# Layer norm statistics of the convolution summed as columns, with filler products between the sums and an earlier load of the silu table

## The reference, cut to what matters

```python
def layer_norm(x, g, b):
    xf = x.astype(jnp.float32)
    mu = jnp.mean(xf, axis=-1, keepdims=True)
    var = jnp.mean(jnp.square(xf - mu), axis=-1, keepdims=True)
    y = (xf - mu) * lax.rsqrt(var + EPS)
    return (y * g.astype(jnp.float32) + b.astype(jnp.float32)).astype(x.dtype)

def conformer_conv_module(h, w_in, b_in, w_dw, b_dw, ln_g, ln_b, w_out, b_out):
    u = h @ w_in + b_in
    a, gate = jnp.split(u, 2, axis=-1)
    u = a * jax.nn.sigmoid(gate)
    u = lax.conv_general_dilated(...) + b_dw        # 31 taps, depthwise, causal
    u = jax.nn.silu(layer_norm(u, ln_g, ln_b))
    return u @ w_out + b_out
```

## Time and profile before

| | |
|---|---|
| median of three runs | 2198.0 us |
| profiled execution, device time | 2200.97 us |
| its span, first to last instruction | 2199.2 us |
| TensorE matmul busy | 2184.2 us, 99% |
| VectorE, ScalarE, GpSimd busy | 1406.0, 991.3, 202.9 us |
| mean granted TensorE clock | 0.998 of full |

### The profile page before, as it was taken

How to read it: one execution, slowest core, us unless ns; L and a number is a source line. 1 busy time by engine, 2 the same in 40 slices (tenths; PEclk the granted TensorE clock), 3 DMA queues, 4 the chain that set the end, 5 groups by cost and what they waited for, 6 DMA issues and landing times.

```text
span 2199.2 us, 32498 instructions
## 1 busy us (share of the span) xinstructions
PE 2184.2 (99%) x13012; PEld 1927.1 (88%) x13012; DVE 1406.0 (64%) x1314; ACT 991.3 (45%) x821; POOL 202.9 (9%) x105
## 2 busy tenths in 40 slices
PE   8999999999999999999999999999999999999998
PEld 8999888888888888888888888888888888888887
DVE  6999786555555555557766767675565555555655
ACT  6666554443344433444354344444443344433444
POOL 7999000000000000000000000000000000000000
PEclk9999999999999999999999999999999999999999
DMA  9665456455545465545544435555555554555452
GB/s 247 183 175 168 138 188 221 176 198 190 190 174 208 172 210 177 207 175 184 194 158 145 143 119 207 194 189 191 191 179 203 180 200 175 200 188 188 174 210 77
DMA packets 250043, 400.46 MB, mean 182 GB/s; under 512 B 6407, under 2 KB 72143, under 8 KB 249935
## 3 DMA queue, kind: packets, MB, share of 16 engines
q1 hardware_dynamic: 249406, 398.74, 53.4%
q0 software_dynamic: 352, 0.56, 0.1%
q10 hardware_dynamic: 208, 0.07, 0.0%
HBM read 397.24 MB, written 2.10 MB: 182 GB/s over the span
## 4 chain that ended last, share of the span: by engine, by line
PE 92%; DVE 4%; issue 2%; DVEq 1%; DMA 1%; ACT 0%; SPq 0%; ACTq 0%
PE bank L1281 55%; PE bank L1283 27%; PE bank L1562 4%; DVE bank L932 2%; PE bank L1354 2%; PE bank L1547 1%; PE bank L1624 1%; DMA raw<-in_conv_w_in 1%; DVEq L910 0%; PE bank L1368 0%; DVE bank L926 0%; PE bank L1499 0%; PE bank L1371 0%; DVE bank L913 0%; PE bank L1489 0%
## 5 line engine op out<-in xcount | busy, mean ns | idle before, releaser
L1281 PE MATMUL bank<-x_both,w_hi 128*128 128x512 f32 x3328 | 1159.0, 395 | 0.0
L775 DVE TENSOR_TENSOR w_lo<-raw,w_hi 128x2048 fp32r<-128x2048 f32 x343 | 779.2, 2290 | 528.9 <-ACT w_hi L486 528.7
L486 ACT ACTIVATE w_hi<-raw 128x2048 fp32r<-128x2048 f32 x374 | 707.4, 1909 | 630.0 <-PE bank L1283 601.5
L1283 PE MATMUL bank<-x_both,w_lo 128*128 128x256 f32 x3328 | 923.8, 278 | 0.0
L1281 PEld LDWEIGHTS bank<-x_both,w_hi 128*128 128x128 f32 x3328 | 625.4, 188 | 146.9 <-issue 1.1
L1281 PE MATMUL bank<-h_both,w_hi 128*128 128x512 f32 x1872 | 651.1, 394 | 0.4 <-DVE h_both L976 0.4
L1283 PEld LDWEIGHTS bank<-x_both,w_lo 128*128 128x128 f32 x3328 | 626.2, 188 | 0.1
L1283 PE MATMUL bank<-h_both,w_lo 128*128 128x256 f32 x1872 | 519.5, 278 | 0.0
L1281 PEld LDWEIGHTS bank<-h_both,w_hi 128*128 128x128 f32 x1872 | 351.1, 188 | 82.9 <-issue 0.5
L1283 PEld LDWEIGHTS bank<-h_both,w_lo 128*128 128x128 f32 x1872 | 351.7, 188 | 0.0
L1354 PE MATMUL bank<-x_both,w_hi 128*128 128x256 f32 x960 | 173.2, 283 | 0.0
(11 more groups left out here) (222 smaller groups left out, 1183.0 us busy)
## 6 DMA issues: line engine op xcount, KB each, us to landing
raw<-in_ffn_w_gate_up SPq DMA_DIRECT2D x176, 1024.0 KB, 4.9
raw<-in_ffn_w_down SPq DMA_DIRECT2D x88, 1024.0 KB, 5.1
raw<-in_gla_w_in SPq DMA_DIRECT2D x48, 1024.0 KB, 5.2
raw<-in_conv_w_in SPq DMA_DIRECT2D x32, 1024.0 KB, 6.1
raw<-in_conv_w_out SPq DMA_DIRECT2D x16, 1024.0 KB, 5.2
raw<-in_gla_w_out SPq DMA_DIRECT2D x16, 1024.0 KB, 7.1
x_rows<-in_x SPq DMA_DIRECT2D x4, 512.0 KB, 6.4
out<-out_rows SPq DMA_DIRECT2D x4, 512.0 KB, 3.1
```

What stands on the lines that cost most here:

```text
L486: nc.scalar.activation(w_hi[k][:, :, :], raw[k][:, :, :], ACT.Copy).then_inc(hi_done, 1)
L775: nc.vector.tensor_tensor(w_lo[k][:, :, :], raw[k][:, :, :], w_hi[k][:, :, :].bitcast(F32), ALU.subtract).then_inc(lo_done, 1)
L1281: mm(to, w_hi[k][:, kt, cols], xx[:, :, k0 + kt, :], start=(first and kt == 0), stop=False, skip_group_check=True)
L1283: ins = mm(to[:, 0:T], w_lo[k][:, kt, cols], xx[:, 0, k0 + kt, :], start=False, stop=(last and kt == 3), skip_group_check=True)
```

## The change

- `column_sums` takes the place of the products with ones. The tile is now the stationary operand, in two halves of 128 tokens, and one column of ones is the moving one; each product gives a 128x1 column of token sums. Ahead of the two products come `idle` filler products (default 1, and 0 for the last two sums). The shift becomes a sum of its own with a column of fours.
- Mean, square, variance, root and reciprocal work on 128x2 elements (`ln_cols`).
- Two diagonal matrices (`neg_mean_diag`, `rstd_diag_ln`, each two 128x128 halves) are made on VectorE, and TensorE turns each into a row form again by a product with the 128x128 ones, twice each, into two PSUM banks: one copy is read by VectorE directly, the other is copied to SBUF by ScalarE (`rows_kept`).
- ScalarE issues a one-element silu straight after the root, so that the table is loaded there.
- `join_last(0)` moves two taps earlier; `ln_center(1)` moves ahead of the first scaling; the fillers after the sums are regrouped.

```diff
@@ last convolution tile, and the statistics on VectorE
-                    if n == JOIN_AT + 4 and last:
+                    if n == JOIN_AT + 2 and last:
                         join_last(0)
...
-            nc.vector.scalar_tensor_tensor(out=sq_sum[:, :], in0=shift[:, :], scalar=4.0 * P, in1=y_total,
-                                           op0=ALU.mult, op1=ALU.add).then_inc(mean_done, 1)
+            nc.vector.tensor_scalar(nm, y_total, -1.0 / D, None, ALU.mult).then_inc(mean_done, 1)
             dve.wait_ge(mean_done, 1)
-            nc.vector.scalar_tensor_tensor(out=rstd[:, :], in0=sq_sum[:, :], scalar=1.0 / D ** 2, in1=sq_sum[:, :],
-                                           op0=ALU.mult, op1=ALU.mult).then_inc(mean_done, 1)
+            nc.vector.tensor_tensor(msq, nm, nm, ALU.mult).then_inc(mean_done, 1)
             dve.wait_ge(mean_done, 2)
             dve.wait_ge(stat_done, STAT[1])
-            nc.vector.scalar_tensor_tensor(out=rstd[:, :], in0=sq_total, scalar=1.0 / D, in1=rstd[:, :],
+            nc.vector.scalar_tensor_tensor(out=var, in0=sq_total, scalar=1.0 / D, in1=msq,
                                            op0=ALU.mult, op1=ALU.subtract).then_inc(var_done, 1)
+            for a in range(2):
+                ins = nc.vector.tensor_scalar(neg_mean_diag[:, a * P:(a + 1) * P], ident[:, :], nm[:, a:a + 1], None, ALU.mult)
+            ins.then_inc(mean_diag, 1)
+            dve.wait_ge(root_done, 2)
+            nc.vector.reciprocal(rs, var).then_inc(rstd_done, 1)
+            dve.wait_ge(rstd_done, 2)
+            for a in range(2):
+                ins = nc.vector.tensor_scalar(rstd_diag_ln[:, a * P:(a + 1) * P], ident[:, :], rs[:, a:a + 1], None, ALU.mult)
+            ins.then_inc(ln_diag, 1)
@@ ScalarE
-            nc.scalar.activation(rstd[:, :], rstd[:, :], ACT.Sqrt, bias=eps[:, 0:1]).then_inc(root_done, 1)
+            nc.scalar.activation(ln_cols[:, 2, :], ln_cols[:, 2, :], ACT.Sqrt, bias=eps[:, 0:1]).then_inc(root_done, 1)
+            nc.scalar.activation(rstd_tok[:, 0:1], eps[:, :], ACT.Silu)
+            scalar.wait_ge(rows_done, 2)
+            nc.scalar.activation(sq_sum[:, :], neg_mean_row[1], ACT.Copy).then_inc(rows_kept, 1)
             for t in range(KT):
...
+                if t == 0:
+                    scalar.wait_ge(rows_done, 4)
+                    nc.scalar.activation(rstd[:, :], rstd_row[1], ACT.Copy).then_inc(rows_kept, 1)
@@ TensorE
-            def add_square(square, signal, count, start=False, stop=False):
+            def column_sums(to, tile, start=False, stop=False, by=None, idle=1):
+
+                busy(tap_first[:, 0:P], idle)
+                by = ones[:, 0:1] if by is None else by
+                for a in range(2):
+                    ins = mm(to[:, a:a + 1], tile[:, a * P:(a + 1) * P], by, start=(start and a == 0), stop=stop,
+                             skip_group_check=True)
+                return ins
+
+            def add_square(square, signal, count, start=False, stop=False, idle=1):
 
                 pe.wait_ge(signal, count)
-                return mm(sq_total, ones[:, :], square, start=start, stop=stop)
-
+                return column_sums(sq_total, square, start, stop, idle=idle)
+
+            pe.wait_ge(tap_done, TAP_STEPS * (KT - 1) - LAST_TAPS[0] + 1)
             add_square(sq_late[:, 4, :], y_sq, 4, start=True)
             add_square(sq_late[:, 5, :], y_sq, 5)
+            pe.wait_ge(consts, 21)
+            column_sums(y_total, shift, start=True, by=four[:, :])
             pe.wait_ge(ysum_done, KT - 1)
-            mm(y_total, ones[:, :], y_sum[:, :], start=True, stop=False)
+            column_sums(y_total, y_sum)
             for tile in range(2):
                 add_square(sq_early[:, tile, :], sq_pre, 3)
             pe.wait_ge(join_done, KT)
-            mm(y_total, ones[:, :], act[:, KT - 2, :], start=False, stop=False)
+            column_sums(y_total, act[:, KT - 2, :])
             add_square(sq_late[:, 6, :], y_sq, 6)
             pe.wait_ge(join_done, KT + 2)
-            mm(y_total, ones[:, :], act[:, KT - 1, :], start=False, stop=True).then_inc(stat_done, 1)
-            add_square(sq_late[:, 7, :], y_sq, 7, stop=True).then_inc(stat_done, 1)
-            for signal, count, n in ((var_done, 1, 2), (root_done, 2, 7), (rstd_done, 2, 1), (z_done, 1, 2), (xn_done, KT + 1, 2)):
+            column_sums(y_total, act[:, KT - 1, :], stop=True, idle=0).then_inc(stat_done, 1)
+            add_square(sq_late[:, 7, :], y_sq, 7, stop=True, idle=0).then_inc(stat_done, 1)
+            busy(tap_first[:, 0:P], 4)
+            pe.wait_ge(mean_diag, 1)
+            for row in neg_mean_row:
+                mm(row, ones[:, :], neg_mean_diag[:, :], start=True, stop=True).then_inc(rows_done, 1)
+            pe.wait_ge(ln_diag, 1)
+            for row in rstd_row:
+                mm(row, ones[:, :], rstd_diag_ln[:, :], start=True, stop=True).then_inc(rows_done, 1)
+            busy(slot[1][:, 2, 0:P], 2)
+            for signal, count, n in ((z_done, 1, 2), (xn_done, KT + 1, 2)):
                 pe.wait_ge(signal, count)
                 busy(slot[1][:, 2, 0:P], n)
```

More of the change, by code:

```diff
@@ L141, in trunk @@
         sq_early = sb("sq_early", [P, 8, T], 72 * K)
-        last_diag = [sb(f"last_diag{j}", [P, P], 80 * K + 512 * j) for j in range(sum(LAST_TAPS))]
-        assert sum(LAST_TAPS) <= 18
+        last_diag = [sb(f"last_diag{j}", [P, P], 80 * K + 512 * j) for j in range(18)]
+        last_diag += [sb(f"last_diag{18 + j}", [P, P], 95 * K + 512 * j) for j in range(2)]
+        assert sum(LAST_TAPS) <= len(last_diag)
+        ln_cols = sb("ln_cols", [P, 4, 2], 93 * K)
+        four = sb("four", [P, 1], 93 * K + 64)
+        neg_mean_diag = sb("neg_mean_diag", [P, T], 91 * K)
+        rstd_diag_ln = sb("rstd_diag_ln", [P, T], 92 * K)
         y_sum = sb("y_sum", [P, T], 69 * K)
@@ L182, in trunk @@
         y_last = [slot[1][:, 2, :], slot[1][:, 0, :]]
-        y_total, sq_total = bank[:, 0, 0:T], bank[:, 1, 0:T]
+        y_total, sq_total = bank[:, 0, 0:2], bank[:, 1, 0:2]
+        neg_mean_row, rstd_row = [bank[:, b, 0:T] for b in (4, 6)], [bank[:, b, 0:T] for b in (5, 7)]
         raw_in = [sem(f"raw_in{i}") for i in range(RING)]
@@ L229, in trunk @@
         var_done = sem("var_done")
+        mean_diag = sem("mean_diag")
+        ln_diag = sem("ln_diag")
+        rows_done = sem("rows_done")
+        rows_kept = sem("rows_kept")
         cent_done = sem("cent_done")
@@ L406, in _ @@
             nc.gpsimd.memset(shift_w[:, :], -1.0 / P).then_inc(consts, 1)
+            nc.gpsimd.memset(four[:, :], 4.0).then_inc(consts, 1)
             for c in range(2):
@@ L953, in _ @@
             join_last(1)
+            nm, msq, var, rs = (ln_cols[:, i, :] for i in range(4))
             dve.wait_ge(stat_done, STAT[1] - 1)
-            nc.vector.scalar_tensor_tensor(out=sq_sum[:, :], in0=shift[:, :], scalar=4.0 * P, in1=y_total,
-                                           op0=ALU.mult, op1=ALU.add).then_inc(mean_done, 1)
+            nc.vector.tensor_scalar(nm, y_total, -1.0 / D, None, ALU.mult).then_inc(mean_done, 1)
             dve.wait_ge(mean_done, 1)
-            nc.vector.scalar_tensor_tensor(out=rstd[:, :], in0=sq_sum[:, :], scalar=1.0 / D ** 2, in1=sq_sum[:, :],
-                                           op0=ALU.mult, op1=ALU.mult).then_inc(mean_done, 1)
+            nc.vector.tensor_tensor(msq, nm, nm, ALU.mult).then_inc(mean_done, 1)
@@ L962, in _ @@
             dve.wait_ge(mean_done, 2)
             dve.wait_ge(stat_done, STAT[1])
-            nc.vector.scalar_tensor_tensor(out=rstd[:, :], in0=sq_total, scalar=1.0 / D, in1=rstd[:, :],
+            nc.vector.scalar_tensor_tensor(out=var, in0=sq_total, scalar=1.0 / D, in1=msq,
                                            op0=ALU.mult, op1=ALU.subtract).then_inc(var_done, 1)
-            def ln_center(t):
-                nc.vector.scalar_tensor_tensor(out=act[:, t, :], in0=sq_sum[:, :], scalar=-1.0 / D, in1=act[:, t, :],
-                                               op0=ALU.mult, op1=ALU.add).then_inc(cent_done, 1)
+            for a in range(2):
+                ins = nc.vector.tensor_scalar(neg_mean_diag[:, a * P:(a + 1) * P], ident[:, :], nm[:, a:a + 1], None, ALU.mult)
@@ new lines, in _ @@
+            ins.then_inc(mean_diag, 1)
[5 more added lines that the diff above has]
+            ins.then_inc(ln_diag, 1)
+            def ln_center(t):
+                if t == 0:
+                    dve.wait_ge(rows_done, 1)
+                if t == 3:
+                    dve.wait_ge(rows_kept, 1)
+                nc.vector.tensor_tensor(act[:, t, :], act[:, t, :], neg_mean_row[0] if t < 3 else sq_sum[:, :],
+                                        ALU.add).then_inc(cent_done, 1)
@@ L971, in _ @@
             ln_center(0)
-            invert(1, rstd[:, :])
+            ln_center(1)
             def ln_remainder(t):
@@ L980, in _ @@
                 dve.wait_ge(cent_done, t + 1)
```

(9 more changed lines are left out.)

## The result

| | before | changed |
|---|---|---|
| median, 21 executions each | 2198.0 us | 2200.84 us |
| ratio, with its 95% interval | | 1.0014 (1.0008 to 1.0019) |
| profiled execution, device time | 2200.97 us | 2200.88 us |
| its span | 2199.2 us | 2199.1 us |
| D: start of tile 15's join to the first output product | 7.08 us | 9.38 us |

The change makes the kernel slower by 2.8 us by the medians (1.8 to 4.2 by the interval of the ratio). That is less than the 0.2% that was called a difference worth telling, but clear of zero, and 2200.84 lies outside the predicted 2196.2 to 2200.4. The forecast was 0.7 us.

A forecast was written before the change was run, and what follows sets the result against it. TensorE, busy for 99% of the span, was taken as the bound, so a later first output product shifts the end. +0.66 us of late scaling and +0.04 of copy made +0.7, 2198.7 us; range 2196.2 to 2200.4, clock left out.

The forecast's parts named there:

- TensorE's queue: Ahead of tile 15: eight sums of six 0.112 us passes delay its sum; scaling 0.66 us late; chance 0.60.
- Rival 2: Between 218 and 226 us: one-column products let TensorE's clock fall to half, about +5 us, 2203 us; chance 0.05.
- The fillers stand against it, and the queue is denser than today's: Sums between 218 and 226 us: the prediction's argument against a falling clock, which was given a chance of 0.05.
- 1.00 throughout this stretch: Layer norm before the change: granted clock 1.00, even from 218.30 to 220.40 with products busy 1.14 of 2.10 us.
- Early table load: ScalarE behind the root: loading silu's table early gains nothing, since today's load already starts right behind the root.
- Rival 1: Sums ahead of tile 15: queue keeps up, scaling 1.16 us earlier, 2196.8 us; chance 0.17 including nearly keeping up.
- Copy between tiles 0 and 1: ScalarE's copy of the mean's second row, some 0.4 us: no stall at the output product, 0 to 0.15, taken 0.04 us.
- Tile 14's earlier join: End of the convolution: the join comes two taps earlier, which nobody waits for.

The follow-up runs named there:

- wide_sums: Changed kernel with 128 equal moving columns in place of one in each column sum: 2198.12 against 2196.29 us before the change, ratio 1.0008; D 7.83 us.
- changed: First profile of the changed kernel as described, against the kernel before: span 2199.1 against 2199.2 us, D 9.38 against 7.08 us.
- changed_look_5: Fifth profile of the unaltered changed kernel: span 2199.5 us, D 11.01 us, clock low for 6.83 us in the layer norm.
- wide_late_load: wide_no_filler without the one-element silu behind the root: 2196.26 us in one run, D 6.79 against 6.12 us.
- wide_no_filler: Changed kernel with 128 moving columns and no fillers between the sums: 2194.66 against 2196.29 us before the change, ratio 0.9992; D 6.12 us.
- wide_rows_first: wide_no_filler with both reciprocal-root rows ahead of the mean's second row, copied after tile 1: 2197.15 against 2196.52 us before the change, ratio 1.0001.

## Why the prediction was wrong, point by point

- **TensorE's queue: right.** The term of D was 0.66 us, later sums less what the small operations give; measured 0.75 (`wide_sums`). Pace of a pass, start of tile 15's sum (2.20 us after its join's start against 2.32 worked out), idle time of VectorE (2.40 for 2.4) all came as worked out, and doubling the fillers moved D by 1.78 for 1.79. The Trainium skill ("TensorE: Matmul & The Clock Gate", LDWEIGHTS) gives columns over 1.2 in ns for a weight load, 107 ns for 128; the measured 0.111 us a pass is within 4% of it. By the figure of the same page of the Trainium skill for 1 to 64 moving columns (Back-to-back issue gap, some 60 cycles) alone, a one-column sum would have taken an estimated 0.10 us; it took 0.45.
- **The clock: the step that failed.** The sum of the prediction has no term for TensorE's clock. Rival 2 stood in the text with its place (between 218 and 226) and its mechanism, but with a chance of 0.05 and outside the range. It happened in every profile of the changed kernel and cost 1.55 us in the first profile: with the 0.75 measured for the rest, that is the 2.30 us of D. The sentence that failed is "The fillers stand against it, and the queue is denser than today's". I took the density of the queue, that is a busy share, as a measure of what keeps the clock. The runs show otherwise: TensorE busy for 2.00 of 2.00 us and a falling clock with one moving column (`changed`), the same passes at the same pace and a steady clock with 128 (`wide_sums`); without fillers, D 9.22 against 6.12 us. No row that I had showed one-column products in number at full clock, so nothing stood behind a chance as low as 0.05.
- **Its price: too high.** I gave about +5 us in all, 4.3 of it clock, for a fall near 219 that lasts until 226. That very case came in `changed_look_5` (219.2 to 226.0): D is 3.93 us above before, 3.2 of it clock. With a low stretch of 3.41 us the clock cost 1.55. Not all work behind the fall is on the chain: root and reciprocal take the same 0.30 and 0.17 us at either clock, and part of the low time covers filler products that nobody waits for. The slower side by over 0.2% did not come in the first timing (ratio 1.0014), but the second gave 1.0024 (1.0014 to 1.0034), so a chance of 0.04 was low for it, and the range needed this case.
- **"1.00 throughout this stretch" was true and hid something.** Elsewhere in the same profile of before the clock fell for 6.83 us (1094.5 to 1101.3), and the granted clock over the whole span would have shown that products which keep TensorE busy throughout (4.00 of 4.00 us, 5.00 of 5.00) can still lose it.
- **Early table load: wrong.** "The early table load gains nothing" compared with before only. Against the copy which the change adds, it is worth 0.67 us (one profile, `wide_late_load` against `wide_no_filler`; not measured in the changed kernel itself).
- **Rival 1's price: nearly right,** 1.16 worked out and 0.96 measured (`wide_no_filler`). The variance came 1.75 us after the join's start for 1.57, which is nearly all of the difference; 0.08 of it lies between tile 15's sum and that of its square (0.53 us for 0.45).
- **Copy between tiles 0 and 1: no stall** in the changed kernel, as taken (the fifth pair of products starts 0.35 us after the fourth); in `wide_rows_first`, with two copies, it came.
- **Tile 14's earlier join: no effect seen,** as taken: the join ends at 214.30, and its sum starts only at 218.60, with no wait noted. No run leaves the move out.
- **Slips that changed nothing.** The chain's steps follow each other within 0.14 us, not 0.1 (the remainder ends at 224.75, the output product starts at 224.89). Two passes in 0.43 us are 0.215 each, not 0.213. Half the spread of the runs is 1.0 us, and the range's lower end takes off 0.6.

## What to carry to other kernels

Where products with few moving columns follow each other, don't go by the busy share of TensorE: read the granted clock. If it falls, try a wider moving operand of the same values. Here 128 columns in place of one cost no time (0.67 us a sum with its filler either way) and kept the clock. Fillers between the products lengthen an in-order queue (here by 1.71 us of D), and their cost falls due where the queue is late already. Of these kernels the one with 128 moving columns and no fillers between the sums has the lowest median (2194.66 us) and, but for one, the shortest D. Compare two kernels by the distance between two events around the change in several profiles, not by the spans of one profile each: here the spans agreed to 0.1 us with 2.3 us of difference inside.

## What the runs showed of the hardware

- One-column float32 passes and 128-column ones run at the same pace, 0.111 to 0.113 us, each with a load of 128x128 weights; at the lower clock a one-column sum of four passes takes 0.86 us (`changed_look_5`) instead of 0.45, so this pace slows down with the clock too.
- The same program loses the clock for 3.41 or for 6.83 us in the layer norm from execution to execution (three and two of five profiles), and near 1094 us for 0, 3.41 or 6.83 us.
- The low stretch near 1094 us cost 0, 1.6 to 1.9 or 3.5 us by execution, as much as most of the differences studied here.
